# A second attention with token-major values, queries and keys projected half a turn ahead, and output rows multiplied inside the last heads

## The reference

```python
k = apply_partial_rope((hk @ w_k).reshape(B, S, 8, 2, 64), cos, sin)
v = (hk @ w_v).reshape(B, S, 8, 128)
q = apply_partial_rope((h @ w_q).reshape(B, S, 8, 2, 64), cos, sin)
# per head, per block of 128 queries, causal:
s = einsum('bqhcd,bkhcd->bhcqk', qi, k) * scale   # two components c
p = softmax(where(kpos <= qpos, s, NEG_INF))
o = (p[:, :, 0] - lam * p[:, :, 1]) @ v
o = rms_norm(o, subln, eps=1e-5) * (1.0 - lam_init)
y = o.reshape(B, S, 1024) @ w_o
```

## Time and profile before

| | us |
|---|---|
| median of 3 runs | 1502.16 (1500.59 to 1502.26) |
| the profiled execution | 1501.49 |
| its span, first to last instruction | 1499.7 |
| PE busy | 1420.3 (95%) |
| DVE busy | 897.5 (60%) |
| ACT busy | 580.4 (39%) |
| POOL busy | 137.0 (9%) |
| mean granted clock of TensorE | 0.975 of full |

### The profile page before, as it was taken

The page is one execution under the profiler, slowest core; times in us unless marked ns, Lnnn a source line. Parts: engine busy times, 40 slices in busy tenths (PEclk is TensorE's granted clock), DMA queues, the critical chain, the costliest instruction groups (busy, mean ns, idle before and its releaser), DMA issues.

```text
span 1499.7 us, 19056 instructions
## 1 busy us (share of the span) xinstructions
PE 1420.3 (95%) x7264; PEld 1173.1 (78%) x7271; DVE 897.5 (60%) x1539; ACT 580.4 (39%) x1003; POOL 137.0 (9%) x218
## 2 busy tenths in 40 slices
PE   4998999999899999999998998897899999999998
PEld 3888888888688788878887776775678888887886
DVE  7777777774468777754557757666157644443223
ACT  4532344345443334331127454555244333332112
POOL 1001000000111111100112000100031000000000
PEclk9999999999999999999999999998799999999999
DMA  9437333230146656544641222211125432333321
GB/s 335 140 88 235 113 96 115 85 99 27 30 144 204 186 171 186 184 147 140 186 151 43 67 61 56 56 56 43 42 70 156 126 98 85 97 99 99 91 92 70
DMA packets 174804, 171.40 MB, mean 114 GB/s; under 512 B 5270, under 2 KB 148999, under 8 KB 174727
## 3 DMA queue, kind: packets, MB, share of 16 engines
q1 hardware_dynamic: 160368, 119.59, 26.7%
q0 software_dynamic: 13824, 50.34, 10.3%
q10 hardware_dynamic: 534, 0.41, 0.1%
HBM read 168.22 MB, written 2.10 MB: 114 GB/s over the span
## 4 chain that ended last, share of the span: by engine, by line
PE 77%; issue 12%; DVE 5%; ACT 2%; POOL 2%; DMA 1%; SPq 0%; POOLq 0%; ACTq 0%; DVEq 0%
PE ps L587 20%; PE ps L519 15%; PE ps L521 14%; PE ps L520 14%; PE ps L853 3%; PE ps L817 2%; PE ps L746 2%; PE ps L562 2%; PE ps L573 1%; DMA mraw<-in_mod_ffn_w_dram 1%; POOL small L2240 1%; PE ps L874 1%; PE ps L637 1%; DVE macc L1668 1%; PE ps L581 1%
## 5 line engine op out<-in xcount | busy, mean ns | idle before, releaser
L1550 DVE TENSOR_TENSOR wlo<-raw,whi 128x1024 fp32r<-128x1024 f32 x206 | 251.3, 1222 | 258.8 <-ACT whi L1108 258.6
L519 PE MATMUL ps<-hhi,whi 128*128 128x512 f32 (+1 forms) x1016 | 395.3, 389 | 4.4 <-DVE hlo L1618 4.4
L521 PE MATMUL ps<-hhi,wlo 128*128 128x512 f32 (+1 forms) x1016 | 387.4, 381 | 0.0
L520 PE MATMUL ps<-hlo,whi 128*128 128x512 f32 (+1 forms) x1016 | 385.9, 380 | 0.0
L1108 ACT ACTIVATE whi<-raw 128x1024 fp32r<-128x1024 f32 x206 | 216.4, 1052 | 271.5 <-PE ps L587 196.3
L519 PEld LDWEIGHTS ps<-hhi,whi 128*128 128x128 f32 x1016 | 192.0, 189 | 41.3 <-issue 6.3
L521 PEld LDWEIGHTS ps<-hhi,wlo 128*128 128x128 f32 x1016 | 191.7, 189 | 37.8
L520 PEld LDWEIGHTS ps<-hlo,whi 128*128 128x128 f32 x1016 | 192.0, 189 | 36.6 <-issue 1.0
L1668 DVE SCALAR_TENSOR_TENSOR macc<-mraw,csil,macc 128x256 f32<-128x256 f32 x294 | 142.3, 484 | 12.9 <-DMA mraw<-in_mod_ffn_w_dram 3.8
L587 PE MATMUL ps<-whi,ghi 128*128 128x512 f32 x352 | 110.9, 396 | 1.7 <-DVE tmp L2014 1.7
L587 PE MATMUL ps<-wlo,ghi 128*128 128x512 f32 x352 | 110.5, 395 | 0.0
(11 more groups left out here) (238 smaller groups left out, 2025.9 us busy)
## 6 DMA issues: line engine op xcount, KB each, us to landing
mraw<-in_mod_ffn_w_dram POOLq DMA_DIRECT2D x48, 512.0 KB, 4.1
raw<-in_ffn_w_gate_dram SPq DMA_DIRECT2D x44, 512.0 KB, 3.8
raw<-in_ffn_w_up_dram SPq DMA_DIRECT2D x44, 512.0 KB, 3.8
raw<-in_ffn_w_down_dram SPq DMA_DIRECT2D x44, 512.0 KB, 3.6
mraw<-in_mod_mix_w_dram POOLq DMA_DIRECT2D x32, 512.0 KB, 3.9
raw<-in_a_w_qkv_dram SPq DMA_DIRECT2D x28, 512.0 KB, 4.2
mstart<-in_mod_mix_w_dram SPq DMA_DIRECT2D x8, 1024.0 KB, 15.0
mraw<-in_kv_mod_w_dram POOLq DMA_DIRECT2D x16, 512.0 KB, 3.8
```

Of the source, the lines that this page charges most:

```text
L519: pe.matmul(out_, whi[:, slot, cols], rhs_hi, start=first, stop=False)
L520: pe.matmul(out_, whi[:, slot, cols], rhs_lo, start=False, stop=False)
L521: return pe.matmul(out_, wlo[:, slot, cols], rhs_hi, start=False, stop=last)
L1550: dve.tensor_tensor(wlo[:, slot, :], raw[:, slot, :], head, ALU.subtract).then_inc(*at.here(lo_ready, ahead))
```

## The change

Layer 1's attention is written anew. The values of four heads at a time are multiplied token-major (the tokens are the stationary operand, 512 columns of `b_w_v` the moving one) in four banks, before the heads; they are read once by ACT into `vB` and are never turned. A head's q is projected in the first half of the head before it and its k in the second half of the one before that; heads are unrolled, with two sets of q and k. The four query tiles form three groups (tiles 0 and 1 together, 2, 3) with two pairs of score banks. The maximum is taken by the same kind of operation as in layer 0: it adds the mask, writes the negated masked scores to SBUF and leaves the maximum, and ACT's exponential works in place in SBUF. The mask matmuls are gone. All turned tiles use one bank (5), read by ACT (probabilities) or by ACT and then DVE (outputs). The normalised output is scaled on ACT; POOL does both steps of the mean square. Where the last two heads have nothing to project, PE multiplies output rows (`lead_of_b`); rows 3 to 7 of `b_w_o` are split into areas of `khi`, `klo`, `hhi`, `hlo` that are no longer read. The gain is spread before the heads, and the output products are ordered so that token tiles 0 and 1 are finished first.

In layer 0 a pair begins with half a projection (`part(0)`, in the last pair `last_values(0)`) ahead of its first scores, the third call of `pair_columns` moves behind pair 0's first scores, the last pair's turned outputs, splits of rows and `lead_of_a` move forward, row 3 of `a_w_o` is split into buffers of its own, and `output_of_a` finishes token tiles 0 and 1 first, as above.

The diff, cut (eight leading spaces are left out; DVE's and ACT's splits of rows, the buffers and the signals are not shown):

```diff
+GROUPS = ((0, 1), (2,), (3,))
+V_BANKS = (2, 3, 4, 7)
+def score_banks(head, group):
+    return (2, 3) if (head + group) % 2 == 0 else (4, 7)
...
+def row_of_b(k, slots):
+    if k < 3:
+        return whi[:, slots[k], :], wlo[:, slots[k], :]
+    a, j = ((khi, klo), 2 * (k - 3)) if k < 7 else ((hhi, hlo), 0)
+    return tuple(part[:, j:j + 2, :].rearrange("p a n -> p (a n)") for part in a)
...
+    load_values_b(0)
+    load_k(0)
+    load_q(0)
+    load_values_b(1)
+    load_k(1)
+    for head in range(1, HEADS_B):
+        load_q(head)
+        if head + 1 < HEADS_B:
+            load_k(head + 1)
     load_rows(b_w_o[0], HEADS_B)
...
         if proj:
+            part(0)
             scores_pair(0)
-            part(0)
             part(1)
+            if pair == 0:
+                pair_columns(4, 2)
             for p in range(CLASSES):
                 turn_prob(p, 0)
                 part(p % 2 if p < 3 else 1)
...
             at.passed("vout", NT)
+            last_values(0)
             scores_pair(0)
-            last_values(0)
...
             last_values(3)
+            turn_o(0, 1)
             values(1, 0, -4)
             scores_pair(3)
             pair_columns(14, 2)
             values(1, 1, -3)
             turn_prob(2, 0)
-            turn_o(0, 1)
+            lead_of_a(1, 0)
             turn_o(1, 0)
             turn_prob(2, 1)
             values(2, 0, -4)
             pe.wait_ge(*at.done(maxed, 7))
             turn_o(2, 4)
-            lead_of_a(1, 0)
+            lead_of_a(1, 1)
             values(2, 1, -2)
             turn_prob(3, 0)
...
-        products(late, 0).then_inc(*at.here(chunk_used))
-        products(early, 2)
-        products(late, 1).then_inc(*at.here(chunk_used, 1))
         pe.wait_ge(*at.done(lo_ready, 3))
-        products(0, 3).then_inc(*at.here(y_done))
+        for t in (0, 1):
...
+        for k in range(2 if early == 2 else 0, 4):
+            mm = products(2, k)
+            if early == 3 and k == 1:
+                mm.then_inc(chunk_used.sems[0], 2)
+        mm.then_inc(*at.here(y_done))
         at.passed("ydone")
-        products(1, 3).then_inc(*at.here(y_done))
-        at.passed("ydone")
-        if late == 2:
-            products(2, 2).then_inc(*at.here(chunk_used, 2))
-        products(2, 3).then_inc(*at.here(y_done))
-        at.passed("ydone")
+        for k in range(2 if early == 3 else 0, 3):
+            mm = products(3, k)
+            if k:
...
+    def enter_b():
+        pe.wait_ge(*at.done(n_ready, 0))
+        for c in range(3):
+            pe.wait_ge(*at.done(lo_ready, c))
+            values_b(0, c, (0, 1))
+            if c == 0:
+                turn_x(2)
+                turn_x(3)
+        pe.wait_ge(*at.done(n_ready, 2))
+        for c in range(3):
+            values_b(0, c, (2, 3)).then_inc(*at.here(chunk_used, c))
+        at.passed("chunk", 3)
+        pe.wait_ge(*at.done(lo_ready))
+        values_b(0, 3, range(NT)).then_inc(*at.here(chunk_used))
+        at.passed("chunk")
+        at.passed("vout", NT)
+        pe.wait_ge(*at.done(m_summed, -1))
+        columns_of([macc[:, j, :] for j in range(4)] + [macc_late[:, j, :] for j in range(2 * PAIRS_LATE - 4)])
+        for diag in (tmp[:, 0, :], tmp[:, 1, :]):
+            spread_gain(diag)
+        part_of_b(1, 0)
+        part_of_b(1, 1)
+        pe.wait_ge(*at.done(n_ready, 3))
+        part_of_b(0, 0)
+        part_of_b(0, 1)
+        for c in range(DT // 2):
+            pe.wait_ge(*at.done(lo_ready))
...
+    def scores_b(head, group):
+        if group == 0:
+            pe.wait_ge(*at.done(qk_lo, 2 * head + 1))
+        if head or group == 2:
+            pe.wait_ge(*at.done(b_maxed, 4 * head + (-2, -1, 1)[group]))
+        qh, ql, kh, kl = qk_odd if head % 2 else qk_even
+        banks = score_banks(head, group)
...
+            for i, (q, k) in enumerate(((qh, kh), (qh, kl), (ql, kh))):
                 for comp in range(2):
-                    mm = pe.matmul(sc[:, comp, n * P:L], identb[:], causal[:, 3 * P:T], start=False, stop=True)
-                mm.then_inc(*at.here(s_ready))
-                at.passed("unit")
...
-    token_stage(ohi1, olo1, HEADS_B, (tmp[:, 0, :], tmp[:, 1, :]), turn_last=turn_last_of_b, lead=2)
+                    r = slice(comp * HEAD_DIM, (comp + 1) * HEAD_DIM)
+                    mm = pe.matmul(ps[:, banks[comp], unit_cols(n)], q[r, tile_cols(n)], k[r, 0:(n + 1) * P],
+                                   start=(i == 0 and n == GROUPS[group][0]), stop=(i == 2), skip_group_check=True)
+        mm.then_inc(*at.here(s_ready))
+        at.passed("group")
...
+    def turn_b(head, group):
+        pe.wait_ge(*at.done(b_read, -1))
+        pe.wait_ge(*at.done(joined, 4 * head + GROUPS[group][-1]))
+        src = prob1[:, (head + group) % 2, 0, :]
+        for e in range(3 if group < 2 else 4):
+            ins = pe.transpose(ps[:, 5, tile_cols(e)], src[:, tile_cols(e)], identf[:])
+        ins.then_inc(*at.here(b_turned))
...
+    def values_of(head, group, jobs=1):
+        pe.wait_ge(*at.done(b_read, -jobs))
+        if head or group:
+            pe.wait_ge(*at.done(b_out, 4 * head + GROUPS[group][0] - 1))
+        for j, n in enumerate(GROUPS[group]):
+            first = unit_cols(n).start // P
+            for e in range(n + 1):
+                mm = pe.matmul(ps[:, 6, tile_cols(j)], aprobT[:, (head + group) % 2, tile_cols(first + e)], vB[:, head, e, :],
+                               start=(e == 0), stop=(e == n))
...
+    def fill(head, quarter):
+        if head < HEADS_B - 2 or head == HEADS_B - 2 and quarter < 2:
+            part_of_b(quarter // 2, quarter % 2)
+        elif head == HEADS_B - 2:
+            if quarter == 2:
+                pe.wait_ge(*at.done(pair_free, -2))
+                lead_of_b(0, 0, range(4))
+        elif quarter == 0:
+            pe.wait_ge(*at.done(pair_free, -1))
+            lead_of_b(0, 1, range(4))
+        elif quarter == 1:
+            for k in (4, 5):
+                for half in range(2):
+                    lead_of_b(0, half, (k,))
+        else:
+            if quarter == 2:
+                pe.wait_ge(*at.done(b_maxed, 4 * head + 2))
+            for half in range(2):
+                lead_of_b(1, half, (0, 1) if quarter == 2 else (2, 3))
+    enter_b()
+    for head in range(HEADS_B):
+        scores_b(head, 0)
+        if head:
+            values_of(head - 1, 2)
+        fill(head, 0)
+        scores_b(head, 1)
+        turn_b(head, 0)
+        fill(head, 1)
+        if head:
+            turn_out_b(head - 1)
+        scores_b(head, 2)
+        fill(head, 2)
+        values_of(head, 0, 2 if head else 1)
+        turn_b(head, 1)
+        fill(head, 3)
+        values_of(head, 1)
+        turn_b(head, 2)
...
+        for half in range(2):
+            lead_of_b(1, half, (4, 5))
+        values_of(HEADS_B - 1, 2)
+        for t in (0, 1):
+            for half in range(2):
+                lead_of_b(t, half, (6,))
+        turn_out_b(HEADS_B - 1)
+        pe.wait_ge(*at.done(b_out, 4 * HEADS_B - 1))
+        pe.wait_ge(*at.done(b_maxed, 4 * HEADS_B - 1))
+        products(3, 0)
+        products(3, 1)
+        pe.wait_ge(*at.done(b_read, -1))
+        pe.wait_ge(*at.done(lo_ready, 7))
...
+            at.passed("ydone")
+        for k in range(HEADS_B):
+            mm = products(2, k)
+            if k < 2:
+                mm.then_inc(*at.here(chunk_used, k))
+        mm.then_inc(*at.here(y_done))
+        at.passed("ydone")
+        for k in range(2, HEADS_B):
+            if k == HEADS_B - 1:
+                turn_x(0)
...
+    def exp_b(head, n):
+        group = 0 if n < 2 else n - 1
+        act.wait_ge(*at.done(b_maxed, 4 * head + n))
+        for comp in range(2):
+            src = prob1[:, (head + group) % 2, comp, unit_cols(n)]
+            ins = act.activation(src, src, ACT.Exp, scale=-1.0, bias=nmaxB[:, n, comp:comp + 1], accum_out=den[:, n, comp:comp + 1])
+        ins.then_inc(*at.here(b_exped, 4 * head + n))
...
+    def out_b(head, group):
+        act.wait_ge(*at.done(b_pv, 3 * head + group))
+        for j, n in enumerate(GROUPS[group]):
+            act.activation(oraw[:, n, :], ps[:, 6, tile_cols(j)], ACT.Copy, scale=rden[:, n, 0:1]).then_inc(*at.here(b_out, 4 * head + n))
+        for n in GROUPS[group]:
+            act.wait_ge(*at.done(b_out, 4 * head + n))
+            act.activation(squares, oraw[:, n, :], ACT.Square, accum_out=osum[:, 0, n:n + 1]).then_inc(*at.here(o_square, 4 * head + n))
+            act.wait_ge(*at.done(o_square, 4 * head + n))
+    def norm_b(head, n):
+        act.wait_ge(*at.done(o_rms, 4 * head + n))
+        act.activation(osb1[:, n, :], oraw[:, n, :], ACT.Copy, scale=osum[:, 2, n:n + 1]).then_inc(*at.here(o_normed, 4 * head + n))
...
+    for head in range(HEADS_B):
+        exp_b(head, 0)
+        exp_b(head, 1)
+        if head:
+            out_b(head - 1, 2)
+        if head < HEADS_B - 1:
+            chunk()
+        read_turned_b(head, 0)
```

(114 more changed lines are left out.)

475 lines of the change are left out of this document (223 added, 252 removed).

## The result

The changed kernel takes **1462.84 us** (median of 4 runs, 1462.31 to 1465.85) where the kernel before, on the same chip, takes 1502.21: a ratio of 0.974, 95% interval 0.973 to 0.976. It is faster, within the range, but the gain is 39.4 us where 54.7 were forecast. The profiled execution spans 1461.1 us, 38.6 less than before.

The account below looks back on a forecast made before the run. PE was taken to carry each head's turn (busy 24.95 us of 27.68). 1501.49 - 39.7 (stage) - 0.5 (tail) - 14.5 (layer 0) = 1446.8 us profiled, forecast median 1447.5, range 1435 to 1472.

Parts of the forecast that it names:

- The stage: Layer 1's attention, first product to last `turn_x`: from 302.0 us to 262.3, a gain of 39.7 us.
- Entry: Layer 1's attention before head 0: 15.4 us unchanged, then 59.5 for values, columns, the gain's spread and first projections.
- The three chains between 18.3 and 18.6 us: Layer 1's heads: PE, DVE and ACT chains nearly equal; with imperfect meshing 19.0 us a head, 27.68 before.
- the prediction's reading of the lock: Layer 1's heads: tile 2's POOL power, shut out by DVE, would begin up to 1.1 us late in every head.
- Layer 0: First attention: pair starts, first-pair wait and output rows together gain 14.5 us, between 5 and 19.
- the first pair's 6.0: Layer 0, pair 0: the 3.58 us wait for a modulation sum and a low-clock stretch go, 6.0 us.
- the starts' 4.5: Layer 0's other three starts: earlier dense matmuls may bring the clock back earlier, 1.5 us each, 4.5 in all.
- The 4.0 for the output rows: Layer 0's `output_of_a`: tiles 0 and 1 finished earlier remove a 3.12 us wait and half-clock `turn_x`, 4.0 us.
- Heads of 22 to 24 us: Rival, layer 1's heads: DVE's chain, not PE, sets the turn; 23 us a head, 1470 us in all; chance 0.20.
- The clock: Rival "slower", layer 1's heads: waits drop PE to 1.2 GHz, 16 us more in eight heads, 1575 us; chance 0.05.
- 9 to 10: Rival, layer 0 gives little: 9 to 10 us of gain go, 1457 us; chance 0.14 shared with the last heads.
- The last heads' rows: Rival, layer 1: output rows wait for splits, head 7 10 us longer, 1457 us; chance 0.14 shared with layer 0.

Follow-up runs that it names:

- e12: e5 with ScalarE's scaled outputs of tile 2 and read of the last turned tiles ahead of normalising tiles 0 and 1; 1437.75 us, ratio 0.956.
- e6: The kernel before with 192 unused bytes per partition behind `mixf`, putting the activations at 105856; 1489.93 us, ratio 0.991.
- e5: The changed kernel with 96 unused bytes per partition behind `osum`, putting the activations at 105856; 1439.28 us, ratio 0.958.
- e10: e5 with the output products that fill heads 6 and 7 moved behind the last head; 1448.80 us, ratio 0.965.
- e11: e5 with the two mask-and-maximum operations of the longest unit of each head done twice; 1451.23 us, ratio 0.966.
- e8: e5 with layer 0's one job of modulation columns moved back from the first pair to behind the first projection's last values; 1444.98 us, ratio 0.960.
- e7: e5 with first scores again ahead of the projection's first part in layer 0's three pairs that project the next; 1443.15 us, ratio 0.960.
- e9: e5 with the last pair and output rows of layer 0 as before the change; 1439.81 us, ratio 0.958.
- m1: Kernel without the trunk, running both 512-column product patterns alone with one operand shifted by 0 to 480 bytes; 0.2271 to 0.2346 us per product.

## Why the prediction was right in its sign and too high in its size

- **The stage** was to last 262.3 us and lasted 264.6. Entry: 74.9 forecast, 78.55 measured, for two low stretches where the sum had one (the spread's). Head 0: 17.5, measured 16.67. Heads 1 to 5: 19.0 each, 95.0; measured 93.00. Head 6: 21.3, measured 20.53. Head 7 and what is left: 19.6 + 34.0 = 53.6, measured 55.81 at a clock of 0.95. The errors, 0.8 to 3.7 us each, go both ways and nearly cancel: that the sum is off by only 2.3 us is in part luck.
- **The three chains between 18.3 and 18.6 us** were right: 18.44, with DVE 89% busy, and the 0.6 for imperfect meshing was too much. The mask-and-maximum of all sizes costs 3.3 us a head, as taken: 0.61 us at 512 columns and about 0.21 at 128, start to start, far from its upper bound. The sentence that POOL's power can stand in ACT's way held: 1.00 us beside a DVE operation with both operands in SBUF, 0.55 otherwise. The Trainium skill, "SBUF — State Buffer", section "Who interferes with whom", tells of that lock; here the power beside such an operation takes 0.45 us longer, and with ACT's wait for POOL taken out (e12) a head gains 0.34, where the prediction's reading of the lock had up to 1.1.
- **Layer 0**: 14.5 forecast, 11.5 measured. Its terms were not too high. With both kernels at their best place the FFN starts at 414.69 us in e6 and at 397.18 to 399.31 in the four profiles that have e5's layer 0 (e5, e10, e11, e12), 15.4 to 17.5 earlier. What the changed kernel lacks is again the slower products, 576 of the first pattern in layer 0: its FFN starts at 402.36, 3 to 5 us behind those four. Term by term, the first pair's 6.0 and the starts' 4.5 stand beside 5.7 and 3.9 by the medians of e8 and e7. The 4.0 for the output rows, with the last pair taken at 0, stands beside 3.5 to 5.5 by e9's trace and 0.5 by its median.
- **The tail**: 0.5 forecast, none measured (8.90 us from `turn_x(1)` to the FFN in both).
- **The step that failed by most** is the sentence "Everything outside layer 1's attention and layer 0's is the same in both kernels". The code is; the addresses are not. The term was 0 and measured 10.4 us (5.1 + 5.3) in the two FFNs. In the profiled execution the missing 16.1 us (54.7 - 38.6) are these 10.4, 3.0 of layer 0, 2.3 of the stage and the tail's 0.5 (rounded). The 3.0 have the same cause.
- **The rivals.** Heads of 22 to 24 us did not come, though their mechanism, a chain through DVE, is what sets the 18.4. The clock did not fall in the heads; it fell where PE really idled (e10: 0.78). Layer 0 gave 3 us less, not 9 to 10. The last heads' rows did come in time.

## What to carry to other kernels

Before costing an edit at nothing for unchanged code, look whether it adds or removes a tensor: compare the stride of the commonest matmul in both traces, start to start, and place the streamed and the stationary operand the same distance from a multiple of 256 bytes. When a loop's period stays the same while its busiest engine gets quicker, it is a loop of waits: lengthen one step of it to see if the period grows by as much, then look for the in-order engine that waits for something its successor does not need. When runs of one kernel scatter by more than a part is worth, compare the length of the stretch in which the part acts, in several traces, and not the whole time of one against one.

## What was not expected of the hardware

A fp32r product of 512 columns takes 0.227 to 0.228, 0.229 or 0.232 to 0.235 us by the rest by 256 bytes of the difference between its operands' addresses, with other engines still or busy (m1); on these kernels that is worth 12 to 24 us, though in the first attention and the heads rest 0 brings 0.229 and not 0.227. And the same code is granted 1.00 in one execution and 0.92 in another behind the same short waits (81.22 and 87.33 us of one entry). In layer 0 the order of a pair's start changed how often that happens: 10 low stretches at 10 places with the old order, 4 at 16 with the new.
